# Dense weights laid with row 128k+p on partition p, and a normalised copy written in the order in which it is read

## The chip, the cores and the metric

The kernel runs on one core of one Trainium2 chip. The metric is the device time of one execution in microseconds (us), the median of three runs.

## The reference

A two-layer encoder trunk over x of 512 rows by 1024 columns, all in float32. With `norm(x, g) = x * rsqrt(mean(x*x) + eps) * g`:

```
x = x + sgu(norm(x, a_norm))                # z = gelu(h @ a_w_in + b); u, v = split(z); v mixed in blocks of 128 rows; (u*v) @ a_w_out
x = x + moe(norm(x, m_norm[0]))             # 32 experts, two for each row
k, v, f = split(norm(x, kv_norm) @ kv_w)    # heads of 64, keys normalised, f gives cumulative log forget sums
q, gate = split(norm(x, b_norm) @ b_w_qg)
x = x + (attention(q, k, v, f) * sigmoid(gate)) @ b_w_out
x = x + moe(norm(x, m_norm[1]))
```

There are five norms. The results of three of them ("a", "kv" and "b") go into dense products with `a_w_in` (1024 x 4096), `kv_w` (1024 x 2064) and `b_w_qg` (1024 x 2048). The results of the other two ("m0" and "m1") go to the router and to the experts.

## The kernel before

The five engines have instruction streams written out by hand, tied by semaphores. X stays in SBUF as four blocks of 128 rows, each 128 partitions by 1024 columns.

**A norm for a dense product.** ScalarE (`block_stats`, L506 to L510) sums the squares of a block and takes the root. VectorE (`scaled_rows`, L726 to L743) takes the reciprocal (L734), and one scalar_tensor_tensor (L739) writes X times that scalar times the gain into one of two buffers, `hrow`, laid as [partition, k, q] with k of 8 and q of 128. It reads X and the gain through the pattern `(q k) -> k q`, so consecutive elements read lie 8 floats (32 bytes) apart, while the result is written in one contiguous run. Slot (k, q) thus holds column 8q+k. TensorE (`transpose_dense_rows`, L1091 to L1100) turns each 128-column piece, two groups of four for a block. ScalarE copies the turned group out of PSUM, rounded (`transposed_rows`, L524), and VectorE writes the remainder (`rows_lo`, L749): each float32 value is split in two parts, and a product is three matmuls (`split_product`, L1075 to L1077). Partition q of chunk k then holds row 8q+k of the operand.

**Dense weights.** They pass through a ring of two buffers in tiles of 1024 rows by 512 columns, 2 MB each, issued from SP's queue in `load_tile` (L319), two of them at L381. In `rows_pk` (L268) partition p gets the rows 8p to 8p+7; each row's piece is 2 KB in DRAM, and successive pieces of a partition lie one weight row apart. Sixteen of the 22 tiles are laid so; the six of `a_w_out` and `b_w_out` go through `rows_cp` (L271), where row 128k+p is on partition p. ScalarE rounds a tile in four pieces (`split_hi`, L532) and VectorE subtracts (`split_lo`, L757). The 16 forget-gate columns of `kv_w` are loaded once by POOL (L469) with the row order of `rows_pk`.

**Order around the three norms.** In "a" VectorE runs the scaled rows of block t and then `rows_lo` of block t-1; after block 3 it splits tile 0. ScalarE's stats of block t+1 stand ahead of its copies of block t. In "kv" VectorE's queue holds `combine` of block t+1 (two scalar_tensor_tensors, L873, which add two gathered expert rows, each scaled, to X) ahead of the scaled rows of block t. TensorE turns blocks 0, 1 and 2, starts the first product, and turns block 3 after it. In "b" the blocks 0 and 1 are scaled during the value projection and the blocks 2 and 3 after it; two pairs of PSUM banks serve the four blocks (L292), so the turn of block t waits for `rows_lo` of block t-2. After the four turns come 20 small matmuls for the cumulative sums (L1361, L1362), four turns of their result (L1366) and the query projection.

"m0" and "m1" use the same `scaled_rows` with another destination, `h_tok` in H, in the same permuted order; the router weights and the experts' w1 and w3 are laid for that order.

Of the kernel before, what the change touches and what calls it, by code (L numbers as in the profile page):

```python
# [20 lines left out]
ALU = mybir.AluOpType  # L21
# [3 lines left out]
P = 128  # L25
D = 1024
T = 512
NT = T // P
KD = D // P
EPS = 1e-6  # L30
WIDTH = 2 * D
NC = WIDTH // P
SG = 8
HEADS = 16
# [17 lines left out]
COL = 512  # L52
# [4 lines left out]
def trunk(nc, x_in, a_norm, a_w_in, a_b_in, a_v_norm, a_w_s, a_b_s, a_w_out, kv_norm, kv_w, kv_b_f, k_norm,  # L57
          b_norm, b_w_qg, q_norm, b_w_out, m_norm, m_w_group, m_b_group, m_w_expert, m_b_expert,
          m_w1, m_w3, m_w2, out):
    with ExitStack() as ctx:  # L60
        def sb(name, shape, dt=F32):
            return ctx.enter_context(nc.sbuf_tensor(name, shape, dt))
# [18 lines left out]
        X = sb("X", [P, NT, D])  # L81
# [3 lines left out]
        gain = sb("gain", [P, D])  # L85

        h_tok = H[:, :].rearrange("p (t k q) -> p t k q", t=NT, k=KD)
# [31 lines left out]
        def scr(a, b):  # L119
            return SCR[:, a:b]  # L120

        hrow = [scr(s * D, (s + 1) * D).rearrange("p (k q) -> p k q", k=KD) for s in range(2)]
# [46 lines left out]
        rinv = sb("rinv", [P, NT])  # L169
# [10 lines left out]
        wf = sb("wf", [P, KD, HEADS])  # L180
# [84 lines left out]
        stored = sem("stored")  # L265


        def rows_pk(w, c0):  # L268
            return w.rearrange("(p k) n -> p k n", k=KD)[:, :, c0:c0 + COL]

        def rows_cp(w, c, c0):  # L271
            return w[c * KD * P:(c + 1) * KD * P, c0:c0 + COL].rearrange("(k p) n -> p k n", p=P)

        tiles = [rows_pk(a_w_in[0], WIDTH + COL * i) for i in range(4)]
        tiles += [rows_pk(a_w_in[0], COL * i) for i in range(4)]
        tiles += [rows_cp(a_w_out[0], c, COL * n) for n in range(2) for c in range(2)]
        tiles += [rows_pk(kv_w, COL * i) for i in range(4)]
        tiles += [rows_pk(b_w_qg[0], COL * i) for i in range(4)]
        tiles += [rows_cp(b_w_out[0], 0, COL * n) for n in range(2)]
        T_V, T_U, T_O, T_K, T_VV, T_Q, T_G, T_WO = 0, 4, 8, 12, 14, 16, 18, 20  # L280

# [118 lines left out]
        def _(pool):  # L400
# [64 lines left out]
            for i, src in enumerate((k_norm, q_norm[0])):  # L465
                for h in range(2):
                    pool.dma_start(cols_raw[2 * NC + i:2 * NC + i + 1, h * DH:(h + 1) * DH],
                                   src.rearrange("(a p) -> a p", a=1)).then_inc(col_loaded, 16)
            pool.dma_start(wf[:, :, :], kv_w.rearrange("(p k) n -> p k n", k=KD)[:, :, 2 * D:2 * D + HEADS])\  # L469
                .then_inc(col_loaded, 16)  # L470
            pool.dma_start(bf_bc[:, :], kv_b_f.partition_broadcast(P)).then_inc(col_loaded, 16)
            for i in range(4):
# [243 lines left out]
        def _(dve):  # L716
            v = nc.vector
            done = [0]

            def then(ins):  # L720

                done[0] += 1
                ins.then_inc(dve_step, 1)
                dve.wait_ge(dve_step, done[0])

            def scaled_rows(n, dst, stats=True, combine=None, after=None, blocks=range(NT)):  # L726
                m = norm[n]
                dve.wait_ge(m["gain"], 16)
                for t in blocks:
                    if combine is not None:  # L730
                        combine(t)
                    if stats:
                        dve.wait_ge(m["rms"], t + 1)
                        then(v.reciprocal(rinv[:, t:t + 1], rms[:, t:t + 1]))  # L734
                    if dst is hrow and t >= 2:

                        dve.wait_ge(m["tr"], 2 * t - 2)
                    to = hrow[t % 2] if dst is hrow else h_tok[:, t]
                    v.scalar_tensor_tensor(to, X[:, t, :].rearrange("p (q k) -> p k q", k=KD), rinv[:, t:t + 1],  # L739
                                           gain[:, :].rearrange("p (q k) -> p k q", k=KD), ALU.mult, ALU.mult)\  # L740
                        .then_inc(m["hrow"], 1)
                    if after is not None and t >= 1:
                        after(t - 1)  # L743

# [123 lines left out]
            def combine(l, t):  # L868

                m = moe[l]  # L870
                dve.wait_ge(m["y_got"][t], 32)
                for k in range(2):
                    v.scalar_tensor_tensor(X[:, t, :], y_got[:, 2 * t + k, :], w12[:, 4 * k + t:4 * k + t + 1],  # L873
                                           X[:, t, :], ALU.mult, ALU.add).then_inc(m["combined"], 1)
                    dve.wait_ge(m["combined"], 2 * t + k + 1)
# [3 lines left out]

            v.memset(vss[:, :, :], 0.0).then_inc(z_ready, 1)  # L880
            scaled_rows("a", hrow, after=lambda t: rows_lo("a", t))
            split_tile(0)
            rows_lo("a", NT - 1)
# [57 lines left out]
            for t in range(NT):  # L941
                add_mixed(0, t)
            split_tile(T_O + 3)

            add_mixed(1, 0)
            scaled_rows("m0", h_tok, combine=lambda t: add_mixed(1, t + 1))
            moe_dve(0)


            split_tile(T_K)  # L950

            combine(0, 0)
            scaled_rows("kv", hrow, combine=lambda t: combine(0, t + 1) if t + 1 < NT else None,
                        after=lambda t: rows_lo("kv", t))
            rows_lo("kv", NT - 1)
# [50 lines left out]
            for u in range(n_units + 4):  # L1006
                if u < n_units:
                    i, c = u % NT, u // NT
                    w = (i + 1) * P
# [16 lines left out]
                q = u - (PAIRS // 2 * NT + 3)  # L1026
                if 0 <= q < 4:
                    split_tile(T_WO, q, q + 1)
                if 1 <= u <= n_units:
                    q = u - 1  # L1030
                    dve.wait_ge(p_exp, 2 * q + 2)
                    then(v.reciprocal(rrec[:, q % 3, :], rsum[:, q % 3, :]))
                    w = (q % NT + 1) * P
# [4 lines left out]
                if 2 <= u <= n_units + 1:  # L1038
                    q = u - 2
                    i = q % NT  # L1040
# [422 lines left out]
```

## Time and profile before

| | |
|---|---|
| median of three runs | 1740.22 us (1738.03 to 1741.03) |
| profiled execution | 1743.63 us, its span 1741.9 us |
| TensorE busy | 1463.7 us, 84% of the span |
| weight load into TensorE busy | 973.3 us, 56% |
| VectorE busy | 606.9 us, 35% |
| ScalarE busy | 329.6 us, 19% |
| mean granted TensorE clock | 0.933 of full speed |
| moved by DMA | 488.02 MB, 280 GB/s over the span |

The span runs from the first to the last instruction of the execution that the hardware profiler recorded. PE is TensorE's matmuls and PEld its weight loads, DVE is VectorE, ACT ScalarE, SP the engine that issues most transfers; SPq or ACTq is such an engine's DMA queue. Names such as SCR, EB or H are buffers of the program (`hrow` lies in SCR, the weight ring and its rounded copies in EB). "Idle before it <-X" names what ended the idle time of an engine ahead of an instruction. The stages lie at: norm "a" 6 to 25 us, gating unit to 285, first expert layer to 806, norm "kv" 816 to 845, key and value projections to 944, norm "b" 939 to 958, then queries, attention and the second expert layer.

### The profile page before, as it was taken

Reading aid. Unit: us, or ns where it says so; the run is one execution under the profiler, and the core shown is the slowest. Engines: PE = TensorE matmul, PEld = TensorE weight load, DVE = VectorE, ACT = ScalarE, POOL = GpSimd, SP = SyncE. Lnnn points to the kernel's source line nnn. Section 1 sums busy time; section 2 is a strip of 40 time slices with the busy share of each in tenths; the row PEclk is TensorE's granted clock in tenths of the full one; section 3 lists DMA queues with packets and bytes.
Section 4 is the critical chain, followed back from the end, with each engine's and each line's share of the span. In section 5 each row is a group of like instructions: output and inputs, shape, how many; then the busy total and the mean of one; then the engine's idle time right before and its main releaser. Section 6 shows DMA issues by size and latency. Waiting matters only on the chain.

```text
span 1741.9 us, 39107 instructions
## 1 busy us (share of the span) xinstructions
PE 1463.7 (84%) x15941; PEld 973.3 (56%) x15942; DVE 606.9 (35%) x1356; ACT 329.6 (19%) x669; POOL 35.0 (2%) x62
## 2 busy tenths in 40 slices
PE   6999999698987989772898979987888899966653
PEld 4888888455554655431787834456455556533331
DVE  5247522422222322214535346744222222211113
ACT  5441312100000000002331334522000000000000
POOL 2100000000000000001000000000000000000001
PEclk9999999799999999976889999999899999988886
DMA  5621225899999999997113122056699998999994
GB/s 195 219 99 49 97 97 226 321 395 423 425 422 423 421 421 417 427 422 285 58 53 109 50 84 85 25 193 266 264 412 423 422 405 322 407 422 423 421 420 158
DMA packets 101155, 488.02 MB, mean 280 GB/s; under 512 B 10656, under 2 KB 22800, under 8 KB 84464
## 3 DMA queue, kind: packets, MB, share of 16 engines
q1 hardware_dynamic: 76544, 457.19, 64.7%
q10 hardware_dynamic: 20528, 17.10, 3.1%
q0 software_dynamic: 4032, 13.01, 2.3%
q8 instruction: 37, 0.61, 0.1%
q14 instruction: 14, 0.11, 0.0%
HBM read 468.61 MB, written 18.64 MB: 280 GB/s over the span
## 4 chain that ended last, share of the span: by engine, by line
issue 46%; PE 26%; DMA 21%; ACTq 3%; DVE 3%; ACT 1%; POOL 1%; SPq 0%; POOLq 0%; DVEq 0%
DMA y_rows<-SCR 12%; DMA EB<-in_m_w 8%; PE ps L1075 7%; PE ps L1077 7%; PE ps L1076 7%; ACTq L582 3%; PE ps L1202 2%; DVE SCR L739 1%; PE ps L1272 1%; DMA EB<-y_rows,pos_i 1%; PE ps L1217 1%; DVE X L873 1%; PE ps L1346 1%; POOL EB L454 1%; PE ps L1184 1%
## 5 line engine op out<-in xcount | busy, mean ns | idle before, releaser
L1202 PE MATMUL ps<-EB,SCR 128*32 128x256 f32 x6016 | 382.8, 411 | 122.8 <-DMA EB<-in_m_w 94.9
L1202 PEld LDWEIGHTS ps<-EB,SCR 128*32 128x32 f32 x6016 | 218.9, 118 | 280.3 <-issue 193.1
L853 DVE TENSOR_TENSOR SCR<-SCR,ps 64x256 f32<-64x256 f32 x94 | 39.7, 423 | 611.3 <-ACT SCR L570 611.3
L1077 PE MATMUL ps<-EB_r 128*128 128x512 f32 x512 | 202.3, 395 | 0.0
L1184 PE MATMUL ps<-H,SCR 128*32 128x256 f32 x3072 | 187.7, 384 | 6.4 <-DVE SCR L784 6.4
L1217 PE MATMUL ps<-EB,SCR 128*32 128x256 f32 x3008 | 184.0, 385 | 2.3 <-issue 0.2
L575 ACT ACTIVATE SCR<-ps 128x256 f32 (+1 forms) x94 | 36.1, 384 | 593.9 <-issue 440.6
L1184 PEld LDWEIGHTS ps<-H,SCR 128*32 128x32 f32 x3072 | 108.4, 111 | 66.4 <-issue 9.3
L1217 PEld LDWEIGHTS ps<-EB,SCR 128*32 128x32 f32 x3008 | 105.4, 110 | 54.9 <-issue 20.2
L1075 PE MATMUL ps<-EB_r,H_r 128*128 128x512 f32 x320 | 129.3, 404 | 1.3 <-DVE EB L890 0.9
L1076 PE MATMUL ps<-EB_r,H_r 128*128 128x512 f32 x320 | 126.9, 396 | 0.0
L1076 PE MATMUL ps<-EB_r 128*128 128x512 f32 x320 | 125.1, 391 | 0.0
L757 DVE TENSOR_TENSOR EB_r<-EB,EB_r 128x1024 fp32r<-128x1024 f32 x80 | 92.8, 1219 | 50.5 <-ACT EB_r L532 50.5
L1077 PEld LDWEIGHTS ps<-EB_r 128*128 128x128 f32 x512 | 97.8, 191 | 21.1
L532 ACT ACTIVATE EB_r<-EB 128x1024 fp32r<-128x1024 f32 x80 | 78.3, 1047 | 85.3 <-DMA EB<-in_a_w_out 44.1
L570 ACT ACTIVATE SCR<-ps 64x256 f32<-64x256 f32 x94 | 35.4, 377 | 271.7 <-PE ps L1202 270.9
L1075 PE MATMUL ps<-EB_r 128*128 128x512 f32 x192 | 75.7, 394 | 2.0 <-DVE EB_r L1050 2.0
L1075 PEld LDWEIGHTS ps<-EB_r,H_r 128*128 128x128 f32 x320 | 61.9, 193 | 14.6 <-DVE EB L890 1.3
L1398 PE MATMUL ps<-H,EB 128*128 128x512 f32 x128 | 64.0, 624 | 6.8 <-DVE H L1013 6.1
L1076 PEld LDWEIGHTS ps<-EB_r,H_r 128*128 128x128 f32 x320 | 61.9, 193 | 12.5
L1076 PEld LDWEIGHTS ps<-EB_r 128*128 128x128 f32 x320 | 60.5, 189 | 12.6
L832 DVE COPY SCR<-ps 128x256 f32<-128x256 f32 x96 | 40.8, 425 | 74.6 <-PE ps L1184 74.0
(197 smaller groups left out, 1318.9 us busy)
## 6 DMA issues: line engine op xcount, KB each, us to landing
EB<-in_m_w SPq DMA_DIRECT2D x192, 2048.0 KB, 10.1
EB<-in_a_w_in SPq DMA_DIRECT2D x8, 2048.0 KB, 10.7
y_rows<-SCR ACTq DMA_DIRECT2D x376, 32.0 KB, 5.9
EB<-in_a_w_out SPq DMA_DIRECT2D x4, 2048.0 KB, 7.9
EB<-in_kv_w SPq DMA_DIRECT2D x4, 2048.0 KB, 15.3
EB<-in_b_w_qg SPq DMA_DIRECT2D x4, 2048.0 KB, 10.6
y_rows<-X SPq DMA_DIRECT2D x2, 2048.0 KB, 17.4
SCR<-ncum_rows ACTq DMA_DIRECT2D x16, 256.0 KB, 3.7
```

The source lines that it names most:

```text
L532: a.activation(ring_hi[j][:, 2 * q:2 * q + 2, :], ring[j][:, 2 * q:2 * q + 2, :], ACT.Copy)\
L582: act.dma_start(y_rows[bass.ds(n * CAP - CAP, CAP), g * CW:(g + 1) * CW], ysb[g * CAP:(g + 1) * CAP, bass.ds(((n + 1) & 1) * CW, CW)])\
L757: v.tensor_tensor(ring_lo[j][:, 2 * q:2 * q + 2, :], ring[j][:, 2 * q:2 * q + 2, :], ring_hi[j][:, 2 * q:2 * q + 2, :].bitcast(F32), ALU.s ...
L832: v.tensor_copy(xg, ps[1][:, 0:CW]).then_inc(m["xg"], 1)
L853: v.tensor_tensor(hid[0:HALF, :], silu[HALF:P, :], ps[0][HALF:P, 0:CW], ALU.mult).then_inc(m["hid"], 1)
L1075: mm(o, left[0], right[0], start=start, stop=False)
L1076: mm(o, left[0], right[1], start=False, stop=False)
L1077: return mm(o, left[1], right[0], start=False, stop=stop)
L1184: last = mm(ps[1][g * CAP:(g + 1) * CAP, 0:CW], S[:, c, :], H[:, c * D + g * CW:c * D + (g + 1) * CW], start=c == 0, stop=c == NT - 1)
L1202: last = mm(ps[0][g * CAP:(g + 1) * CAP, 0:CW], xT[:, k, :], w[:, k, g % 2 * CW:(g % 2 + 1) * CW], start=k == 0, stop=k == KD - 1)
L1217: last = mm(ps[4][g * CAP:(g + 1) * CAP, 0:CW], hidT[:, c, :], w2_sb[s][:, c, g * CW:(g + 1) * CW], start=c == 0, stop=c == KE - 1)
L1398: last = mm(ps[7][:, :], ring[j % 2][:, k, c % 4 * P:(c % 4 + 1) * P], hT[:, k, :], start=k == 0, stop=k == KD - 1)
```

## The change

The tiles of `a_w_in`, `kv_w` and `b_w_qg` and the forget-gate columns are laid with row 128k+p on partition p of chunk k. For "a", "kv" and "b" the scalar_tensor_tensor reads X and the gain as they lie, so that slot (k, q) holds column 128k+q. "m0" and "m1" keep the permuted order. No instruction, wait or buffer is added or taken away.

```diff
-        def rows_pk(w, c0):
-            return w.rearrange("(p k) n -> p k n", k=KD)[:, :, c0:c0 + COL]
+        def rows_kp(w, c0):
+            return w.rearrange("(k p) n -> p k n", p=P)[:, :, c0:c0 + COL]
...
-        tiles = [rows_pk(a_w_in[0], WIDTH + COL * i) for i in range(4)]
-        tiles += [rows_pk(a_w_in[0], COL * i) for i in range(4)]
+        tiles = [rows_kp(a_w_in[0], WIDTH + COL * i) for i in range(4)]
+        tiles += [rows_kp(a_w_in[0], COL * i) for i in range(4)]
         tiles += [rows_cp(a_w_out[0], c, COL * n) for n in range(2) for c in range(2)]
-        tiles += [rows_pk(kv_w, COL * i) for i in range(4)]
-        tiles += [rows_pk(b_w_qg[0], COL * i) for i in range(4)]
+        tiles += [rows_kp(kv_w, COL * i) for i in range(4)]
+        tiles += [rows_kp(b_w_qg[0], COL * i) for i in range(4)]
...
-            pool.dma_start(wf[:, :, :], kv_w.rearrange("(p k) n -> p k n", k=KD)[:, :, 2 * D:2 * D + HEADS])\
+            pool.dma_start(wf[:, :, :], kv_w.rearrange("(k p) n -> p k n", p=P)[:, :, 2 * D:2 * D + HEADS])\
...
-                    to = hrow[t % 2] if dst is hrow else h_tok[:, t]
-                    v.scalar_tensor_tensor(to, X[:, t, :].rearrange("p (q k) -> p k q", k=KD), rinv[:, t:t + 1],
-                                           gain[:, :].rearrange("p (q k) -> p k q", k=KD), ALU.mult, ALU.mult)\
-                        .then_inc(m["hrow"], 1)
+                    if dst is hrow:
+                        v.scalar_tensor_tensor(hrow[t % 2].rearrange("p k q -> p (k q)"), X[:, t, :], rinv[:, t:t + 1],
+                                               gain[:, :], ALU.mult, ALU.mult).then_inc(m["hrow"], 1)
+                    else:
+                        v.scalar_tensor_tensor(h_tok[:, t], X[:, t, :].rearrange("p (q k) -> p k q", k=KD),
+                                               rinv[:, t:t + 1], gain[:, :].rearrange("p (q k) -> p k q", k=KD),
+                                               ALU.mult, ALU.mult).then_inc(m["hrow"], 1)
```

## Rows read from the trace of the kernel before

**Rows 1.** The page's chain that ended last, shares of the span by line.

```profile
DMA y_rows<-SCR 12%; DMA EB<-in_m_w 8%; PE ps L1075 7%; PE ps L1077 7%; PE ps L1076 7%; ACTq L582 3%; PE ps L1202 2%; DVE SCR L739 1%; PE ps L1272 1%; DMA EB<-y_rows,pos_i 1%; PE ps L1217 1%; DVE X L873 1%; PE ps L1346 1%; POOL EB L454 1%; PE ps L1184 1%
```

**Rows 2.** VectorE's groups by line and shape: busy us, mean ns | idle before.

```profile
L739 DVE SCALAR_TENSOR_TENSOR SCR<-X,rinv,gain 128x1024 f32<-128x1024 f32 x12 | 25.1, 2097 | 0.5 <-PE ps L1098 0.3
...
L873 DVE SCALAR_TENSOR_TENSOR X<-EB,w,X 128x1024 f32<-128x1024 f32 x16 | 20.5, 1284 | 20.3 <-DMA EB<-y_rows,pos_i 20.1
L739 DVE SCALAR_TENSOR_TENSOR H<-X,rinv,gain 128x1024 f32<-128x1024 f32 x8 | 17.6, 2195 | 0.3
```

**Rows 3.** Timeline of 10 to 25 us: start us, us, engine and line [idle before].

```profile
16.74 0.17 DVE L734 RECIPROCAL rinv<-rms 128x1 f32<-128x1 f32 x1 [0.67 <-ACT rms L509]
...
20.31 2.06 DVE L739 SCALAR_TENSOR_TENSOR SCR<-X,rinv,gain 128x1024 f32<-128x1024 f32 x1
...
22.22 3.90 ACT L532 ACTIVATE EB_r<-EB 128x1024 fp32r<-128x1024 f32 x4 [0.56 <-DMA EB<-in_a_w_in]
22.29 1.28 DVE L749 TENSOR_TENSOR EB_r<-ps,H_r 128x512 fp32r<-128x512 f32 x2
...
24.85 0.76 PE L1075 MATMUL ps<-EB_r,H_r 128*128 128x512 f32 x1 [0.45 <-DVE EB_r L757]
```

**Rows 4.** The chain of work from 813 to 838 us: start us, us, what.

```profile
813.28 6.06 DMA EB<-y_rows,pos_i
...
822.30 2.07 DVE SCR L739
...
833.12 2.07 DVE SCR L739
835.24 1.97 PE ps L1098 x8
```

**Rows 5.** Timeline of the norm "kv", three rows.

```profile
818.40 1.02 POOL L454 DMA_INDIRECT EB<-y_rows,pos_i  x1 [0.30 <-issue]
...
819.46 2.61 DVE L873 SCALAR_TENSOR_TENSOR X<-EB,w,X 128x1024 f32<-128x1024 f32 x2 [0.85 <-DMA EB<-y_rows,pos_i]
...
828.10 0.29 ACT L509 ACTIVATE rms<-ss,eps 128x1 f32<-128x1 f32 x1
```

**Rows 6.** VectorE's timeline of the norm "b", after the value projection.

```profile
945.53 2.09 DVE L739 SCALAR_TENSOR_TENSOR SCR<-X,rinv,gain 128x1024 f32<-128x1024 f32 x1 [0.25 <-PE ps L1098]
947.53 1.29 DVE L749 TENSOR_TENSOR EB_r<-ps,H_r 128x512 fp32r<-128x512 f32 x2
948.73 2.08 DVE L739 SCALAR_TENSOR_TENSOR SCR<-X,rinv,gain 128x1024 f32<-128x1024 f32 x1
```

**Rows 7.** TensorE's timeline of the norm "b".

```profile
944.39 1.91 PE L1098 MATMUL ps<-ident,SCR 128*128 128x128 f32 x16
948.37 1.16 PE L1098 MATMUL ps<-ident,SCR 128*128 128x128 f32 x8 [2.08 <-DVE EB_r L749]
951.55 1.94 PE L1098 MATMUL ps<-ident,SCR 128*128 128x128 f32 x8 [2.02 <-DVE EB_r L749]
...
958.56 0.78 PE L1075 MATMUL ps<-EB_r,H_r 128*128 128x512 f32 x1
```

**Rows 8.** Busy time by stretch: the stretch, PE busy, PEclk, DMA share, GB/s.

```profile
950.00:952.00 2.00, 0.45 (x2) 0.59 0.93 310
960.00:962.00 2.00, 2.00 (x9) 0.85 0.08 21
```

**Rows 9.** L319's a_w_in issues, then landings of tile 0, a_w_in, a_w_out, kv_w.

```profile
L319 SPq DMA_DIRECT2D EB<-in_a_w_in x8: 539/542/3904, 3.0 to 176.0; - x8
...
DMA to landing us min/median/max: 19.2/19.2/19.2
...
DMA to landing us min/median/max: 8.1/8.1/8.1
...
DMA to landing us min/median/max: 7.9/7.9/7.9
...
DMA to landing us min/median/max: 10.3/10.3/10.3
```

## The prediction

> **What bounds the kernel now.** I read the page's chain first. It is made of expert loads and stores, of the split products on TensorE, and of one small VectorE entry: L739 in SCR, 1% of the span [rows 1]. That is the instruction which the change rewrites, and only the stretches where it stands in the chain can give anything back. VectorE is busy for 35% of the span, so less work on it is worth nothing by itself. The second view is VectorE's groups by shape: twelve L739 instructions write `hrow` at 2097 ns each, and eight more write H at 2195 ns [rows 2]. The eight stay as they are. The third view is the three places, "a", "kv" and "b", each as a timeline: there the reader should look for what ends the wait of TensorE's first product. The fourth is the landing times of the ring's tiles, since the change lays sixteen of the 22 in another order of DRAM addresses.
>
> **The instruction.** After the change it reads two float32 streams and a scalar for each partition and writes one, all contiguous, 128x1024. The trace has that very form: L873, also a scalar_tensor_tensor of 128x1024 with a scalar for each partition, at 1284 ns [rows 2]. The present form differs from it in the 32-byte step of its reads. I take 1.285 us, against 2.07 in most places of the chain, so 0.79 us less for each. The bounds are no saving at all (the step costs nothing and something else makes L739 slow) and those 0.81 us that the means give, 2097 - 1284. All twelve together are 9.7 us of VectorE, of which most lies beside other work.
>
> The Trainium skill has two rules here that point different ways. "VectorE: DVE Perf Modes", in its part on the 1x baseline mode, says that float32 with odd strides is simply served at one result per cycle; by that alone the saving would be zero and the sum below zero with it. "SBUF — State Buffer", in the section on the DMA port swizzle, says that SBUF is read in 16-byte lines and that an access which enters a new line each time pays; a step of 32 bytes does that. The two rows decide for the second: same operation, same size, 813 ns apart.
>
> **Norm "a".** Blocks 0 to 3 run at 10.6, 12.7, 16.9 and 20.3 us. The third is preceded by an idle 0.67 us that the root of ScalarE ended [rows 3], so part of what the first two give is waited away unless ScalarE's queue moves as well. It does: its copies of block 0 wait for the turned rows, which come 0.8 us earlier, and its stats of block 2 stand behind them. The fourth instruction would then start about 1.4 us earlier and end about 2.2 earlier. But ScalarE then stands at the split of tile 0, and it already waits 0.56 us for the tile's DMA, until 22.2 [rows 3]. That landing does not move with VectorE: issued at 3.0, landed 19.2 us later [rows 9]. Of the gain only this is left: VectorE's subtraction of the first piece now starts at 23.57, when `rows_lo` of block 2 is over, while ScalarE's first piece is ready at about 23.25 (22.22 plus a quarter of 3.90 and some 0.06). So the first product, now at 24.85, comes 0.3 us earlier. From there on the six matmuls for each pair of chunks run at the low clock and take longer than VectorE's piece (its four follow ScalarE's, 3.90 us for four), and nothing else is late. **Gain 0.3 us**; bounds 0 and 0.6.
>
> **Norm "kv".** Here VectorE itself is the chain. The pattern is L739, two L873 of the next combine, L739 and so on: three L739 (822.30, 827.11, 833.12) lie ahead of the turn of block 2 at 835.24, and the first product follows it at 837.21 [rows 4]. Each L739 gives 0.785 us, together 2.36. What is late next? Three things could take its place. The gathered rows: the combine of block 1 waited 0.85 us for its rows [rows 5], ahead of the first L739, and those of blocks 2 and 3 would have to land before about 823.5 and 828.8; with the last of the eight gathers issued at 818.40 [rows 5], the two before it earlier still, and 6.06 us for the gathers in the chain [rows 4], both are there. The roots: ScalarE's root of block 2 ended at 828.4 [rows 5], behind copies that also come earlier, and VectorE wants it at about 831. The split of the first weight tile stands ahead of all combines in VectorE's queue and is over. None of these binds. Block 3's L739 comes after the last chain link and is hidden by the first product. **Gain 2.36 us**; bounds 1.6 (one of the three is waited away) and 2.4.
>
> **Norm "b".** Blocks 0 and 1 are scaled beside the value projection, which ends at 944.4: their gain is hidden by it. Block 2's L739 starts at 945.53 because it waits for TensorE to have turned block 0, which frees its buffer [rows 6]; that doesn't move. It ends 0.8 earlier, so do `rows_lo` of block 0 and block 3's L739, which ends 1.6 earlier, and `rows_lo` of block 1 behind it. TensorE waits twice for just these, 2.08 and 2.02 us [rows 7]. The turn of block 2 starts 0.8 us earlier and that of block 3, now at 951.55, 1.57 earlier (2 x 0.785). After it the queue holds small matmuls and the query projection, which begins at 958.56 with nothing in between that waits long. **Gain 1.57 us**; bounds 0.8 and what the clock may add, below.
>
> **Clock.** In "b" the granted clock falls from 2.4 to 1.2 GHz just before 951 us, after the two idle stretches, and is back at about 961, when the projection had run some 2.4 us [rows 8]. The turn of eight pieces takes 1.94 us at the low level and 1.16 at the high one, waits included [rows 7]. With shorter idle stretches it may fall later or not at all. If it never fell, the work from 951.55 to 961, about 9.1 us of it busy, would take about half, 4.5 us less. I take nothing for it, since TensorE still has two idle stretches over 1 us and then small matmuls; the bounds are -1.5 (the rise comes later against the projection) and 4.5.
>
> **The transfers.** Sixteen tiles keep their 1024 pieces of 2 KB; only the addresses change. The nearest rows for the new order are the tiles of `a_w_out`, landed in 7.9 us where one of `a_w_in` takes 8.1; `kv_w`'s in the old order takes 10.3 [rows 9]. Each tile in mid-stage is issued when its buffer comes free and needed after the other buffer's products; eight issues from 3.0 to 176.0 [rows 9] are 25 us apart, so a landing of 8 or 10 us is hidden, and one of twice that would be. Two places are not covered. Tile 0 is the one of "a", where every us of landing is a us of the result. And the first two `kv_w` tiles are issued as the first expert layer ends and share the DMA engines with its last items' stores, which are in the chain [rows 1]. I take 0 for both, with bounds of -2 (tiles of `kv_w` drop to 8 us) and +5.2 (tile 0 slowed by 10.3/8.1, worked out below). POOL's load of the gate columns has the same 1024 pieces of 64 bytes and is needed only after the key projection: nothing.
>
> **The sum.** 0.3 + 2.36 + 1.57 = 4.2 us. The profiled execution took 1743.63, of which the span is 1741.9; it becomes 1739.4. It stands 3.4 above the median of the runs, so against the median the forecast is 1740.22 - 4.2 = 1736.0.
>
> **Rivals.**
> *The clock joins in* at "b" or comes back earlier somewhere: 1736.0 - 4.5 = 1731.5 at most. For it: the two gaps shrink from 2.1 to about 1.3 us. Against: the matmuls behind them are tiny. Chance 0.13.
> *Part of the gain is waited away*, by a root, a gathered row or a copy of ScalarE in "kv" or "b": a third to a half is lost, 1738. The idle 0.67 in "a" shows such waits exist. Chance 0.15.
> *The step costs nothing*, so that nothing is gained: 1740.2. Against it stand the two rows above. Chance 0.04.
> *Tile 0 lands later* (slower than before). Its pieces on one partition now lie 128 rows of 16,384 bytes apart, 2 MB. If that cost what `kv_w`'s order costs over `a_w_in`'s, 10.3/8.1 = 1.27, the 19.2 us to landing would be 24.4, 5.2 later, and passed on in full; 1740.2 - 3.9 + 5.2 = 1741.5. It decides from 3.9 us of delay on, and is slower by a measurable amount from 7.4, a factor of 1.39. Against it: `a_w_out`'s tiles, with 512 KB between pieces, land as fast as the rest. Chance 0.08, half of it past 7.4.
> The skill's "DMA: Bandwidth & Descriptors", section on latency and other measured facts, bears on that last case: it reports copies with a row pitch of 2 MiB at 164 GB/s where 512 KiB gave 207. No row here has such a pitch; by its ratio, 1.26, an estimate would be the same 5 us.
>
> **How the numbers follow.** A measurement of this kernel can tell about 0.2%, 3.5 us, from no change; the forecast lies 4.2 away, and the three runs spread over 3 us, so the forecast case (0.60) gives "faster" about two times in three. Faster: 0.40 + 0.13 + 0.03 (partly waited away) = 0.56. Slower: 0.04. Same: the rest, 0.40. The range runs from 1732.0, short of the full clock case, to 1739.3, which takes in half the gain lost and the scatter; what is left out is the far clock case, no gain and the late tile.
>
> **What would show it.** L739 in SCR at 1.27 to 1.30 us, in H still at 2.19. In "kv" the stretch from the first L739 to the first product 12.5 us, not 14.9. In "b" idle stretches of about 1.3 us in place of 2.1, and 5.6 us rather than 7.2 from the end of the value projection to the turn of block 3. In "a" the first product still close behind tile 0's landing. Wrong would be L739 near 2.07, a new wait for a root or for gathered rows ahead of L739 in "kv", or tile 0 landing over 1 us later.

## The result and the profile after

The changed kernel took 1734.51 us (median of 8 runs) beside 1740.68 for the kernel before; the ratio is 0.995 with a 95% interval of 0.9937 to 0.9963. (The two medians alone lie 6.2 us apart. The gains below are worked out from the ratios, here and for every experiment.) Put on the 1740.22 us of the forecast, that is 1731.5 us: 8.7 us faster, where 4.2 were forecast, and 0.5 us under the low end of the range. The profiled execution is the quickest of the eight, 1730.19 us with a span of 1728.4, so stretches are compared below and not its end. (Lines after 742 have moved by 3: L1078 to L1080 are the split products, L1101 the turns, L752 `rows_lo`, L876 the combine.)

The combine in VectorE's groups of the changed kernel, columns as in [rows 2]:

```profile
L876 DVE SCALAR_TENSOR_TENSOR X<-EB,w,X 128x1024 f32<-128x1024 f32 x16 | 20.5, 1284 | 20.5 <-DMA EB<-y_rows,pos_i 20.2
```

The view of line 739 (duration in ns: least, median, most; first and last start):

```profile
L739 DVE SCALAR_TENSOR_TENSOR SCR<-X,rinv,gain x12: 1273/1284/1286, 10.5 to 944.2; 128x1024 f32<-128x1024 f32 x12
```

The price taken from the combine's row was right to the nanosecond. Norm "a", ScalarE's and TensorE's timelines, answering to [rows 3]:

```profile
19.45 0.60 ACT L524 ACTIVATE H_r<-ps 128x512 fp32r<-128x512 f32 x1 [0.26 <-PE ps L1101]
22.36 2.00 ACT L532 ACTIVATE EB_r<-EB 128x1024 fp32r<-128x1024 f32 x2 [2.32 <-DMA EB<-in_a_w_in]
...
24.82 0.77 PE L1078 MATMUL ps<-EB_r,H_r 128*128 128x512 f32 x1 [2.82 <-DVE EB_r L760]
```

ScalarE now waits 2.32 us for tile 0 where it waited 0.56: what VectorE saves here ends in that wait. Norm "kv", the chain, answering to [rows 4]:

```profile
823.29 1.29 DVE SCR L739
824.58 1.21 DVE X L876
825.81 1.30 DVE X L876
...
832.56 1.30 DVE SCR L739
833.90 1.97 PE ps L1101 x8
835.87 0.43 PE ps L1078
```

The same links in the same order, each L739 shorter. By this chain the stretch from the first L739 to the first product is 12.58 us, where the prediction had 12.5. Norm "b", TensorE's timeline, answering to [rows 7]:

```profile
940.68 1.91 PE L1101 MATMUL ps<-ident,SCR 128*128 128x128 f32 x16
943.86 1.16 PE L1101 MATMUL ps<-ident,SCR 128*128 128x128 f32 x8 [1.27 <-DVE EB_r L752]
946.25 1.94 PE L1101 MATMUL ps<-ident,SCR 128*128 128x128 f32 x8 [1.23 <-DVE EB_r L752]
...
953.26 0.78 PE L1078 MATMUL ps<-EB_r,H_r 128*128 128x512 f32 x1
```

The idle stretches shrank from 2.08 and 2.02 us to 1.27 and 1.23, as forecast.

What the forecast did not name lies 60 us later, where attention starts. VectorE waits there for the forget sums that ScalarE's queue loads (ncum_rows), and TensorE for the next thing in VectorE's queue, the re-joined h (L1013). First the waits of the kernel before from 990 to 1045 us (in total, times, longest), then those of the changed one:

```profile
DVE SCR L1023 <- DMA SCR<-ncum_rows: 8.1, 1, 8.1
PE ps L1398 <- DVE H L1013: 6.1, 1, 6.1
```

```profile
DVE SCR L1026 <- DMA SCR<-ncum_rows: 5.7, 1, 5.7
PE ps L1401 <- DVE H L1016: 1.0, 1, 1.0
```

That stretch cut in two at the landing of the sums, first before, then after (columns: stretch, its length, busy PE, PEld, DVE, ACT, POOL, then PEclk, DMA share, GB/s):

```profile
1008.10:1018.00 9.90, 3.99 (x20) 1.89 (x20) 1.82 (x2) 2.30 (x3) 0.00 (x0) 1.00 0.93 297
1018.00:1025.40 7.40, 5.63 (x11) 2.02 (x12) 4.04 (x14) 1.97 (x8) 0.00 (x0) 0.54 0.03 11
```

```profile
1003.10:1010.60 7.50, 5.93 (x16) 2.78 (x18) 1.83 (x3) 2.32 (x3) 0.00 (x0) 0.54 1.03 375
1010.60:1015.40 4.80, 3.81 (x17) 1.52 (x18) 4.03 (x14) 1.97 (x8) 0.00 (x0) 1.00 0.14 52
```

The first piece is 2.4 us shorter because the sums land sooner. The second is 2.6 us shorter for the same work of VectorE and ScalarE (14 and 8 instructions) because the granted clock is at 2.4 GHz in it. Before, the low clock (1.2 GHz) followed TensorE's 6.1 us of waiting and fell on the first units of attention; after, it fell into the wait. Together that is 5.0 us, more than the whole forecast.

Why the sums land sooner stands in the rows of the tile that travels beside them, the second gate tile of `b_w_qg`. It is issued 4 to 5 us ahead of the four loads of the sums (from 1010.3 us before, 1005.8 after). Its issue and landing, then the landings of those four loads, for the kernel before and the changed one:

```profile
L319 SPq DMA_DIRECT2D EB<-in_b_w_qg x1: 539/539/539, 1006.2 to 1006.2; - x1
DMA to landing us min/median/max: 11.5/11.5/11.5
DMA to landing us min/median/max: 6.1/6.7/7.3
```

```profile
L319 SPq DMA_DIRECT2D EB<-in_b_w_qg x1: 367/367/367, 1001.2 to 1001.2; - x1
DMA to landing us min/median/max: 8.1/8.1/8.1
DMA to landing us min/median/max: 4.2/4.6/5.0
```

### The profile page after: what moved, and what is told of

It is laid out like the page before. It is cut to its first block, busy times and chain, and to the rows that moved or that the text cites. A ratio compares the mean times of both kernels' runs of the same rounds, so it can differ in the third digit from the quotient of the medians.

```text
span 1728.4 us, 39107 instructions
## 1 busy us (share of the span) xinstructions
PE 1461.3 (85%) x15941; PEld 974.9 (56%) x15942; DVE 597.0 (35%) x1356; ACT 329.5 (19%) x669; POOL 34.8 (2%) x62
## 4 chain that ended last, share of the span: by engine, by line
issue 45%; PE 25%; DMA 23%; ACTq 3%; DVE 2%; ACT 1%; POOL 1%; SPq 0%; POOLq 0%; DVEq 0%
DMA y_rows<-SCR 13%; DMA EB<-in_m_w 8%; PE ps L1078 7%; PE ps L1079 7%; PE ps L1080 7%; ACTq L582 3%; PE ps L1205 1%; DMA EB<-in_a_w_in 1%; PE ps L1275 1%; DMA EB<-y_rows,pos_i 1%; DVE X L876 1%; PE ps L1349 1%; POOL EB L454 1%; PE ps L1220 0%; DVE SCR L739 0%
## 5 line engine op out<-in xcount | busy, mean ns | idle before, releaser
L1080 PE MATMUL ps<-EB_r 128*128 128x512 f32 x512 | 202.8, 396 | 0.0
L1078 PE MATMUL ps<-EB_r,H_r 128*128 128x512 f32 x320 | 129.5, 405 | 3.7 <-DVE EB_r L760 2.8
L1080 PEld LDWEIGHTS ps<-EB_r 128*128 128x128 f32 x512 | 98.4, 192 | 21.1
L1078 PE MATMUL ps<-EB_r 128*128 128x512 f32 x192 | 76.2, 397 | 2.0 <-DVE EB_r L1053 2.0
L1078 PEld LDWEIGHTS ps<-EB_r,H_r 128*128 128x128 f32 x320 | 62.1, 194 | 17.1 <-issue 3.2
L1079 PEld LDWEIGHTS ps<-EB_r,H_r 128*128 128x128 f32 x320 | 62.0, 194 | 12.5
```

The lines of the kernel that those rows point to most:

```text
L1078: mm(o, left[0], right[0], start=start, stop=False)
L1079: mm(o, left[0], right[1], start=False, stop=False)
L1080: return mm(o, left[1], right[0], start=False, stop=stop)
```

## The experiments

Two theories stood at first. **A**: everything comes from VectorE's shorter instruction (with luck of the clock). **B**: some 4 us come from it, and some 5 from a `b_w_qg` tile that shares the DMA engines with the forget sums and leaves them sooner in the new row order. Later **C**: the surplus is only where the clock's low stretches happen to fall.

**e1: the new order alone.** The changed kernel, with L739 made to walk with a step, at the same addresses.

```diff
-v.scalar_tensor_tensor(hrow[t % 2].rearrange("p k q -> p (k q)"), X[:, t, :], rinv[:, t:t + 1], gain[:, :], ...
+v.scalar_tensor_tensor(scr(t % 2 * D, (t % 2 + 1) * D).rearrange("p (q k) -> p k q", k=KD),
+                       X[:, t, :].rearrange("p (q k) -> p k q", k=KD), rinv[:, t:t + 1],
+                       gain[:, :].rearrange("p (q k) -> p k q", k=KD), ...
```

> The changed kernel, but L739 of the three dense norms walks X, the gain and hrow with a step of 8 floats as before, at the same addresses: the new order of the weights alone. Theory A (the whole gain is VectorE's shorter instruction plus a lucky clock): L739 back near 2.1 us, no gain, ratio to the kernel before 1.000. Theory B (two parts: about 4 us from L739 in kv and b, and about 5 us because a tile of b_w_qg in the new order leaves the DMA engines sooner to the loads of the forget sums at the start of attention): ratio about 0.997, a b_w_qg tile landing in about 8 us and not 10.4 to 11.5, VectorE's wait for ncum_rows 5 to 6 us and not 8.1, L739 near 2.1 us.

Ratio 0.9977 (0.9963 to 0.999), 4.0 us. Line 739, and then the waits at the start of attention:

```profile
L739 DVE SCALAR_TENSOR_TENSOR SCR<-X,rinv,gain x12: 2053/2073/2301, 10.6 to 947.0; 128x1024 f32<-128x1024 f32 x12
```

```profile
DVE SCR L1028 <- DMA SCR<-ncum_rows: 6.5, 1, 6.5
PE ps L1403 <- DVE H L1018: 4.5, 1, 4.5
```

The instruction is slow again, the sums are sooner all the same (the tile beside them landed in 8.0 us), and there is a gain. A falls.

**e2: the short instruction alone.** The kernel before with its weights in the old order; L739 contiguous, and TensorE picks every eighth column when it turns.

```diff
+                        v.scalar_tensor_tensor(hrow[t % 2].rearrange("p k q -> p (k q)"), X[:, t, :], rinv[:, t:t + 1],
+                                               gain[:, :], ALU.mult, ALU.mult).then_inc(m["hrow"], 1)
...
-                                                   hrow[t % 2][:, 4 * h + j, :], ident[:, :])
+                                                   scr(t % 2 * D, (t % 2 + 1) * D).rearrange("p (q k) -> p k q", k=KD)[:, 4 * h + j, :],
+                                                   ident[:, :])
```

> The kernel before with its order of weights, but L739 of the dense norms contiguous, and TensorE's turns picking every eighth column of hrow: the shorter instruction alone (unless a turn that reads with a step costs more). Theory A: as the changed kernel, ratio 0.995 to 0.996. Theory B: about 4 us, ratio 0.9976, landing of b_w_qg tiles still over 10 us and the wait for ncum_rows still about 8 us. If the turns are slower for the step, both lose that: 96 pieces now at 0.27 us at the high clock.

Ratio 0.996 (0.9947 to 0.9974), 7.0 us, with 4.5 to 9.2 in the interval: more than the 4.2 of the sum, which lies just outside. The wait for the sums stays as in the kernel before, and the tile beside them takes 11.9 us:

```profile
DVE SCR L1028 <- DMA SCR<-ncum_rows: 8.4, 1, 8.4
PE ps L1404 <- DVE H L1018: 3.6, 1, 3.6
```

The two halves give 4.0 and 7.0 us apart and 8.7 together (a second measurement, e5, has 11.0); the intervals allow a plain sum. So the forecast missed two things: the transfer, and something in the short instruction's own gain (e5 shows what it can be; this run's own profile, the slowest of its eleven executions, does not have it). TensorE's wait is 3.6 us here and not 6.1, though VectorE's is as long as before: more on that at e5.

**e3 and e4: the collision taken away.** SP issues the second gate tile only after the sums of the first two pairs have landed; e3 is the kernel before with it, e4 the changed one.

```diff
+                if i == T_G + 1:
+                    sp.wait_ge(nck_loaded[0], 32)
+                    sp.wait_ge(nck_loaded[1], 32)
                 sp.dma_start(ring[i % 2], tiles[i]).then_inc(tile_loaded[i % 2], 16)
```

> The kernel before, with the second gate tile of b_w_qg issued by SP only once the first two pairs' forget sums have landed; needed some 60 us later. Theory A: nothing, ratio 1.000. Theory B: the loads of the sums land in about 4 us and not 7.7, the wait of 8.1 us for them falls to about 4.5, and with less idle time of TensorE behind it 4 to 7 us are gained, ratio 0.996 to 0.9975.

> The changed kernel with the same later issue of that tile. Theory A: as the changed kernel, ratio to before 0.995 to 0.996. Theory B: what is left of the collision goes too, 1 to 2 us more, ratio 0.994 to 0.995; and it ends near the changed kernel, since both take the same loss away.

e3: 0.9974 (0.996 to 0.9988), 4.5 us from moving one issue; the first four loads of the sums land in 3.3 to 4.0 us. e4: 0.9938 (0.9919 to 0.9957), 10.8 us. The waits for the sums, e3 and then e4:

```profile
DVE SCR L1026 <- DMA SCR<-ncum_rows: 4.5, 1, 4.5
```

```profile
DVE SCR L1029 <- DMA SCR<-ncum_rows: 5.1, 1, 5.1
PE ps L1404 <- DVE H L1019: 0.3, 1, 0.3
```

In e3 TensorE's wait for h is gone from the list altogether.

**e6: the collision made worse.** The changed kernel with a 2 MB store beside the sums.

```diff
                 sp.dma_start(ring[i % 2], tiles[i]).then_inc(tile_loaded[i % 2], 16)
+                if i == T_G + 1:
+                    sp.dma_start(y_rows[SLOTS:SLOTS + T, :].rearrange("(p t) n -> p t n", t=NT), X[:, :, :])\
+                        .then_inc(y_filled, 16)
```

(Two waits on `y_filled` were added ahead of the next writers of X and y_rows.)

> The changed kernel, with a 2 MB store of X to a part of DRAM that nobody reads before the second expert layer issued right behind the second gate tile, so that the loads of the forget sums meet more traffic. Theory B: the wait for the sums grows from 5.7 to 8 us or more and at least the 5 us gained there are given back, ratio 0.997 to 1.000. Theory C: nothing but the store's own time, which lies beside the attention, ratio about 0.995.

```profile
DVE SCR L1029 <- DMA SCR<-ncum_rows: 11.2, 1, 11.2
PE ps L1405 <- DVE H L1019: 6.5, 1, 6.5
```

Ratio 0.9991 (0.9979 to 1.0003): the gain of the change is gone, though the scaled rows still take 1284 ns each. The four loads of the sums landed in 9.6 to 9.9 us. What that place costs is set by what travels beside the sums.

**e7 and e8: the sums loaded early.** They go into the other of their two buffers, ahead of the query projection; e7 is the kernel before with it, e8 the changed one.

```diff
-            head_norms(1, G_Q, 1, QT, {1: T_Q + 1})
             def load_nck(c):
                 for h in range(2):
-                    act.dma_start(nck[:, c % 2, h, :], ncum_rows[2 * c + h].partition_broadcast(P))\
+                    act.dma_start(nck[:, (c + 1) % 2, h, :], ncum_rows[2 * c + h].partition_broadcast(P))\
...
             act.wait_ge(ncum_stored, 16)
-
+            load_nck(0)
+            head_norms(1, G_Q, 1, QT, {1: T_Q + 1})
             act.wait_ge(kn_out, 16)
-            load_nck(0)
             load_nck(1)
...
-                                               in1=nck[:, c % 2, h, 0:w], scale=-1.0, ...
+                                               in1=nck[:, (c + 1) % 2, h, 0:w], scale=-1.0, ...
```

> The kernel before, with the first pair's forget sums loaded into the other buffer, before the query projection, where the queues are empty. Theory B: the wait of 8.1 us is gone, 7 to 9 us faster, ratio 0.995 to 0.996. Theory C: the wait is hidden anyway, ratio 1.000.

> The changed kernel with the same early sums. Theory B: the wait of 5.7 us is gone as well; since the tile's order no longer matters at the start of attention, it should beat the kernel before with early sums by L739's 4 us alone, ratio 0.992 to 0.9935, and beat both kernels of the case. Theory C: ratio 0.995, as the changed kernel.

e7: 0.9965 (0.9947 to 0.9983), 6.1 us, a little short of the 7 to 9 expected. e8: 0.9923 (0.9899 to 0.9947), a median of 1728.93 us beside 1741.84, 13.4 us by the ratio: **the best version of the study**, faster than both kernels. Neither has a wait for ncum_rows left; what VectorE waits for at that place in e8 is TensorE's scores:

```profile
DVE SCR L1025 <- PE ps L1388: 6.9, 6, 3.2
```

Between e7 and e8 the tile's order should no longer matter there, and 7.3 us lie between them where 4 were expected. The intervals are wide enough for either. In the stretches of the table below the two profiles differ by 3.5 us (2.3 and 4.0 gained, 2.8 lost); where the rest lies was not found.

**e5, e10 and e11: the same two kernels profiled again.** e5 and e11 are the changed kernel, e10 the kernel before.

> The changed kernel once more, unaltered, for a second profile and as the measure for its neighbours. Theory B (4 us from L739, 4 to 5 from the collision at the start of attention): ratio 0.9945 to 0.9955, stretch from the first L739 of kv to its first product 12.6 us (14.9 before), stretch from the last query heads to the fourth unit of attention 12 us (17.3 before). Theory C (the surplus over the forecast is where the clock's low stretches happen to fall): another profile shows another split, and no steady gain at the start of attention.

> The kernel before, unaltered, for a second profile. Theory B: the stretch from the last query heads to the fourth unit of attention is again about 17 us, VectorE's wait for the forget sums about 8 us, the b stretch from the third L739 to the first query heads about 22 us. Theory C (the clock's low stretches fell unluckily in the first profile): 13 us in the first of these stretches here too.

> The changed kernel, unaltered, for a third profile. Theory B: the start of attention 12 to 13 us, the wait for the sums about 6 us. The stretch of norm b 18 or 21 us, as the clock stays low for one or for three of its steps.

e5: 0.9937 (0.9915 to 0.9959). e10 and e11 are one execution each, 1746.02 and 1732.24 us. The table has the stretches, in us, read from the timelines of all profiles. "kv" runs from the first L739 to the first product, "b" from its third L739 to the norm of the first query heads (L968), "attention" from the last heads' norm (L968) to the first reduction of the third unit (the expectations call it the fourth):

| | L739 | weights | kv | b | attention |
|---|---|---|---|---|---|
| before, e10 | step | old | 14.57, 14.55 | 22.2, 22.4 | 17.3, 17.6 |
| e1 | step | new | 14.54 | 22.2 | 14.7 |
| e3 | step | old, tile late | 14.57 | 23.5 | 11.3 |
| e7 | step | old, sums early | 14.56 | 22.2 | 8.3 |
| e2 | contiguous | old | 12.22 | 21.3 | 16.4 |
| after, e5, e11 | contiguous | new | 12.23, 12.22, 12.22 | 20.9, 18.2, 18.3 | 12.3, 12.7, 15.3 |
| e4 | contiguous | new, tile late | 12.22 | 18.2 | 11.7 |
| e8 | contiguous | new, sums early | 12.22 | 18.2 | 11.1 |
| e6 | contiguous | new, store beside | 12.22 | 20.9 | 19.2 |

"kv" is worth 2.3 us in every profile (14.54 to 14.57 against 12.22 and 12.23; by the kernels' first profiles 2.34). "b" has two values with the short instruction. In the changed kernel's first profile the clock fell before the turn of block 3, which took 1.94 us (shown above). In e5 it stayed high through that turn and the small matmuls behind it. e5's TensorE timeline, and the clock there (columns as above):

```profile
950.21 1.16 PE L1101 MATMUL ps<-ident,SCR 128*128 128x128 f32 x8 [1.23 <-DVE EB_r L752]
...
952.47 0.82 PE L1364 MATMUL ps<-lf,ones 128*128 128x16 f32 x6
```

```profile
950.20:952.20 2.00, 1.99 (x18) 1.88 (x18) 2.00 (x4) 1.14 (x2) 0.12 (x1) 1.00 1.07 398
954.40:956.40 2.00, 2.00 (x7) 1.57 (x6) 0.00 (x0) 0.59 (x1) 0.00 (x0) 0.56 0.07 16
```

The high clock makes the turn and the 20 small matmuls take about half the time, 2.7 us in all, on top of the 0.9 to 1.3 by which the stretch is shorter without it. It did so in five of the eight profiles with a short L739 (e9 below has 18.3) and in none of the five with the long one. C falls as far as "luck" goes: e10 repeats the first profile of before to 0.3 us at each place. That the shorter waits make the high clock likelier fits thirteen profiles but is not shown by them; no run switches the clock by itself. "Attention" varies by 3 us among like kernels for the same cause (in e11 the clock fell once more, after the wait; in e8 it was low there and in e7 not, which is why e7's 8.3 is under e8's 11.1).

The same profiles say more of the clock at the start of attention. TensorE always stands idle for 2.3 us there, until the last query heads are normed. In all eight profiles with the short L739 the granted clock falls at the end of that idle time or up to 0.8 us behind it, and is low while VectorE waits for the sums; of the five with the long one only e3 has this. TensorE's work then fills part of the wait, so that its own wait is shorter (3.6 us in e2, 6.1 before), which goes with about 1 us of "attention" that e2 gains without the transfer (16.4 against 17.3 and 17.6). The length of TensorE's own wait goes with what follows: after 6.1 to 6.5 us (before, e10, e6) the clock was low for 6.8 us, after 2.3 to 4.5 us (e11, e2, e1) for 3.4, and after 1.9 us or less (the other seven) it stayed high. e2, during the wait, around its end and after it:

```profile
1007.40:1014.00 6.60, 5.84 (x16) 2.43 (x16) 0.40 (x1) 1.97 (x2) 0.00 (x0) 0.50 0.93 294
1014.00:1017.50 3.50, 0.28 (x2) 0.01 (x1) 1.33 (x5) 0.88 (x4) 0.00 (x0) 0.98 0.51 195
1017.60:1021.00 3.40, 3.13 (x4) 1.17 (x4) 2.59 (x9) 1.09 (x4) 0.00 (x0) 0.51 0.00 0
```

Why the first fall comes with the short instruction was not tried and stays open.

**e9: the tiles alone.** Behind the last store of the changed kernel one tile after another is loaded, nothing else moving.

```diff
+            for _ in range(3):
+                landed(sp.dma_start(ring[0], b_w_qg[0].rearrange("(p k) n -> p k n", k=KD)[:, :, 0:COL]))
+                landed(sp.dma_start(ring[0], b_w_qg[0].rearrange("(k p) n -> p k n", p=P)[:, :, 0:COL]))
...
```

> The changed kernel with 24 loads of one 2 MB tile added behind its last store, each after the one before has landed: b_w_qg, kv_w, a_w_in and b_w_out, each in the old row order and in the new, three times over. Their time only lengthens the run (by some 200 us). Theory B1 (the order of the rows alone makes the tile of an 8 KB-row weight slow): b_w_qg and kv_w over 10 us in the old order and near 8 in the new, a_w_in and b_w_out near 8 in both. Theory B2 (the difference came from what else ran beside those tiles in the middle of the kernel): both orders the same for each weight.

The issues and landings of `b_w_qg`, `kv_w` and `a_w_in`, for each the old order and then the new:

```profile
L407 SPq DMA_DIRECT2D EB<-in_b_w_qg x3: 551/551/667, 1731.3 to 1871.0; - x3
DMA to landing us min/median/max: 10.5/10.7/10.8
...
L408 SPq DMA_DIRECT2D EB<-in_b_w_qg x3: 368/368/402, 1742.0 to 1881.8; - x3
DMA to landing us min/median/max: 8.0/8.0/8.1
...
L409 SPq DMA_DIRECT2D EB<-in_kv_w x3: 551/551/557, 1750.1 to 1889.7; - x3
DMA to landing us min/median/max: 10.1/10.2/10.2
...
DMA to landing us min/median/max: 7.8/8.0/8.2
...
L411 SPq DMA_DIRECT2D EB<-in_a_w_in x3: 551/551/551, 1768.5 to 1907.9; - x3
DMA to landing us min/median/max: 7.9/8.0/8.1
...
DMA to landing us min/median/max: 8.3/8.6/8.6
```

B1 holds: the order of the rows alone makes a tile of `b_w_qg` land in 8.0 us and not 10.7, and one of `kv_w` in 8.0 and not 10.2. The expectation missed for `a_w_in`, which is a little slower in the new order (8.6, not 8.0), and for `b_w_out`, which it had near 8 in both and which took 8.7 in the old order and 7.8 in the new.

## Why the prediction was wrong

The direction and the mechanism on VectorE were right, the size was not, and the failed steps are "The transfers" and "Clock".

- **The instruction**: forecast 1.285 us, measured 1.284. Of the two rules weighed there the line rule of the Trainium skill ("SBUF — State Buffer", section on the DMA port swizzle) stands. In e1 the write walks with the step as well, and the instruction took 2073 ns, no more than with stepped reads alone (2074).
- **"a"**: forecast 0.3 us. The first product started at 24.82, before at 24.85; over all thirteen profiles it is 23.9 to 25.2 and follows tile 0's landing, which differs by more than 1 us. The wait moved to the DMA as foretold. From ScalarE's first piece of tile 0 to the first product it is 2.46 us in seven of the eight profiles with the short instruction and 2.47 in the other, and 2.46 to 2.73 in the five with the long one: 0.15 us gained on the mean.
- **"kv"**: forecast 2.36 us, measured 2.34 in the first profiles and 2.31 to 2.35 over all. None of the three possible new waits bound.
- **"b", the waits**: forecast 1.57 us. From the end of the value projection to the turn of block 3 it is 5.57 us (946.25 less 940.68), where it was 7.16: 1.59. Of that 1.3 us are left at the first query heads.
- **"Clock"**: taken as 0, with a rival at 0.13 that held up to 4.5 us. It gave 2.7 us in five of eight profiles. I argued that the turns and small matmuls after the two waits would bring the clock down anyway; they do, but often only behind the small matmuls, which then run at full speed. Such executions may also be why e2 gave more than the sum; its one profile has 21.3 us there and does not show it.
- **"The transfers"**: taken as 0, and this is the larger miss. I had the landing of a `kv_w` tile at 10.3 us against 8.1 [rows 9] and asked only whether the tile itself would be late. It never is; the second gate tile of `b_w_qg` is needed over 60 us on. But it is issued when ScalarE is about to load the forget sums, and those are needed at once. A quicker tile (8.0 or 8.1 us to landing and not 11.5 or 12.0) frees the DMA engines for them: the wait fell from 8.1 and 8.4 us to 5.7, 6.2 and 7.0. And a shorter wait of TensorE kept the clock's low stretch off the work behind it in two of the three profiles. Both together gave 2.0 to 5.3 us in three profiles (e1, the order alone: 2.6 and 2.9 beside the two of before), and about 1 us of it came with the instruction alone (e2).
- **The rival "tile 0 lands later"** did not come: 19.4 us to landing, before 19.2. For a 2 MB step between the pieces of a partition e9 shows 8.6 against 8.0 us, a factor of 1.07. The estimate of 1.26, made from the Trainium skill's "DMA: Bandwidth & Descriptors" (latency and other measured facts), does not fit this access: the pitch of that entry is the one from partition to partition, here 16 KB, and the 2 MB lie between the pieces of one partition. The measurement decides.

Summed from the stretches, with means over the three profiles of the changed kernel: 2.3 (kv), 3.2 (b), 4.0 (attention), 9.5 us, against 8.7 (6.4 to 11.0) and 11.0 (7.1 to 14.8) measured. The range ended 0.5 us short of the result because its low end took in part of the clock case and nothing for a transfer's neighbour.

## What to carry to other kernels

When a change makes a transfer shorter or longer, ask not only when that transfer is needed but what is issued beside it and needed at once: a 2 MB tile with over 60 us of slack lengthened VectorE's wait for the forget sums by nearly 4 us (8.1 and 8.4 us with it, 4.5 without, e3). Load small, urgent data before the large tile or while the queues are empty; on the kernel before, that alone (e7) was worth 6.1 us, more than the change had been forecast to bring, and on top of the change (e8) 2.4 to 4.7. And a wait removed ahead of small matmuls may pay twice, since the clock may then stay up for them.

## What the runs showed of the hardware

- Twelve scalar_tensor_tensors of 128x1024 float32 take 1284 ns each when both streams are contiguous and 2074 when both are read with a step of 32 bytes; stepping the write too adds nothing (2073).
- TensorE reading `hrow` with a step of 32 bytes to turn it (e2) left the "kv" stretch at 12.22 us, the same as with contiguous reads.
- A tile of 1024 pieces of 2 KB took, alone on the DMA engines, 10.7 us (8192-byte rows) or 10.2 us (8256-byte rows) with rows 8p to 8p+7 on partition p, and 8.0 with row 128k+p. With 16,384-byte rows it was 8.0 and 8.6, with 4096-byte rows 8.7 and 7.8. Why the middle pitch is the slow one was not tried and stays open.
- Four 256 KB loads from ScalarE's queue, issued 4 to 5 us behind such a 2 MB tile, landed in 6.0 to 7.6 us with the slow row order (before, e10, e2) and in 4.2 to 6.3 with the quick one (after, e5, e11, e1); without the tile beside them (e3, e4) it was 3.1 to 4.6.
- SP issued such a load of 1024 pieces in 0.37 us in the new order and in 0.55 in the old.
